# Accumulators that take turns: two column tiles of a panel, and two token halves, product by product

## What is computed

```
xn   = RMSNorm(h)
proj = xn @ w_in                 # 2048 x N_IN: three mixers (forgetting attention, gated short
                                 # convolution, gated linear attention) and three gate groups
mix  = sum_i sigmoid(g_i + b_i) * (mixer_i(proj) @ w_i_o)
h    = h + mix @ w_o
u    = causal_dwconv3(RMSNorm(h) @ w_up)          # 2048 x 11264
h    = h + (silu(u_gate) * u_up) @ w_down         # 5632 x 2048
out  = RMSNorm(h)[meta tokens dropped]
```

## Time and profile before

| | |
|---|---|
| median of the runs | 1764.99 us |
| own time of the profiled execution | 1764.8 us |
| its span | 1763.0 us |
| TensorE busy, products | 1752.1 us, 99% |
| TensorE busy, weight loads | 1694.5 us, 96% |
| VectorE, ScalarE, GpSimd busy | 64%, 43%, 9% |
| DMA, mean over the span | 180 GB/s |

### The profile page before, as it was taken

How to read it: one execution, slowest core, us unless ns; L and a number is a source line. 1 busy time by engine, 2 the same in 40 slices (tenths; PEclk the granted TensorE clock), 3 DMA queues, 4 the chain that set the end, 5 groups by cost and what they waited for, 6 DMA issues and landing times.

```text
span 1763.0 us, 34040 instructions
## 1 busy us (share of the span) xinstructions
PE 1752.1 (99%) x13509; PEld 1694.5 (96%) x13509; DVE 1125.3 (64%) x1547; ACT 763.7 (43%) x942; POOL 163.4 (9%) x318
## 2 busy tenths in 40 slices
PE   9999999999999999999999999999999999999998
PEld 8999999999999999999999999999999999888886
DVE  6757667577575554555556687777777777554454
ACT  6634444354354444444444443334444334343433
POOL 4030030300300000000000033321000000000000
PEclk9999999999999999999999999999999999999999
DMA  8656556556556556566655566666555565666564
GB/s 230 181 155 166 165 157 178 161 162 170 143 162 192 179 172 188 175 190 190 191 167 191 178 191 191 203 197 187 182 179 180 182 186 174 223 189 187 187 188 134
DMA packets 304662, 317.48 MB, mean 180 GB/s; under 512 B 13769, under 2 KB 279501, under 8 KB 304461
## 3 DMA queue, kind: packets, MB, share of 16 engines
q1 hardware_dynamic: 296861, 311.01, 58.8%
q0 software_dynamic: 7296, 4.68, 1.4%
q10 hardware_dynamic: 432, 0.79, 0.1%
HBM read 311.10 MB, written 2.11 MB: 178 GB/s over the span
## 4 chain that ended last, share of the span: by engine, by line
PE 99%; DVE 0%; DMA 0%; ACT 0%; SPq 0%; issue 0%; ACTq 0%; DVEq 0%
PE ps L1387 27%; PE ps L1389 27%; PE ps L1388 27%; PE ps L1668 5%; PE ps L1670 5%; PE ps L1669 5%; PE ps L1482 0%; DMA xb<-in_x_dram 0%; PE ps L1504 0%; PE ps L1529 0%; PE ps L1519 0%; PE ps L1520 0%; PE ps L1559 0%; PE ps L1560 0%; DVE xl L908 0%; PE ps L1547 0%
## 5 line engine op out<-in xcount | busy, mean ns | idle before, releaser
L863 DVE TENSOR_TENSOR lo<-raw,hi 128x1024 fp32r<-128x1024 f32 x584 | 711.6, 1231 | 510.2 <-ACT hi L582 507.1
L1387 PE MATMUL ps<-xh,hi 128*128 128x260 f32 (+1 forms) x3328 | 946.0, 284 | 0.2 <-DVE xl L908 0.2
L1389 PE MATMUL ps<-xh,lo 128*128 128x260 f32 (+1 forms) x3328 | 942.0, 283 | 0.0
L1388 PE MATMUL ps<-xl,hi 128*128 128x260 f32 (+1 forms) x3328 | 940.3, 283 | 0.0
L582 ACT CAST hi<-raw 128x1024 fp32r<-128x1024 f32 x584 | 604.4, 1048 | 670.5 <-PE ps L1389 539.5
L1387 PEld LDWEIGHTS ps<-xh,hi 128*128 128x128 f32 x3328 | 626.1, 188 | 1.4 <-issue 0.4
L1388 PEld LDWEIGHTS ps<-xl,hi 128*128 128x128 f32 x3328 | 626.5, 188 | 0.2
L1389 PEld LDWEIGHTS ps<-xh,lo 128*128 128x128 f32 x3328 | 625.5, 188 | 0.0
L1668 PE MATMUL ps<-hi,act_h 128*128 128x512 f32 x350 | 139.6, 399 | 0.0
L1670 PE MATMUL ps<-lo,act_h 128*128 128x512 f32 x350 | 137.9, 394 | 0.0
L1669 PE MATMUL ps<-hi,act_l 128*128 128x512 f32 x350 | 137.2, 392 | 0.0
(11 more groups left out here) (306 smaller groups left out, 1189.4 us busy)
## 6 DMA issues: line engine op xcount, KB each, us to landing
raw<-in_w_in_dram SPq DMA_DIRECT2D x224, 512.0 KB, 3.8
raw<-in_w_up_dram SPq DMA_DIRECT2D x176, 512.0 KB, 4.6
raw<-in_w_down_dram SPq DMA_DIRECT2D x88, 512.0 KB, 4.8
raw<-in_w_o_dram SPq DMA_DIRECT2D x32, 512.0 KB, 3.5
raw<-in_w_in_dram SPq DMA_DIRECT2D x32, 256.0 KB, 3.4
raw<-in_w_a_o_dram SPq DMA_DIRECT2D x16, 512.0 KB, 4.4
raw<-in_w_b_o_dram SPq DMA_DIRECT2D x16, 512.0 KB, 3.3
raw<-in_w_c_o_dram SPq DMA_DIRECT2D x16, 512.0 KB, 3.3
```

Source lines behind the costliest of these rows:

```text
L863: nc.vector.tensor_tensor(lo[:, s, :], raw[:, s, :], hi[:, s, :].bitcast(F32), ALU.subtract).then_inc(lo_ready, 1)
L1387: nc.tensor.matmul(acc, w_hi, mh, start=first and j == 0, stop=False)
L1388: nc.tensor.matmul(acc, w_hi, ml, start=False, stop=False)
L1389: ins = nc.tensor.matmul(acc, w_lo, mh, start=False, stop=last and j == KJ - 1)
```

## The change

The tiles of a column panel take turns: for each row block and each of the three products, first tile 0, then tile 1. The two first panels, which have work between their tiles, keep the old order. In the down projection the two token halves take turns in the same way, for all panels but the last four.

```diff
@@ use_panel
                 s = ph.slot(q)
-                for m in range(2):
-                    if m and between:
+                for j in () if between else range(KJ):
+                    mh, ml = moving(j)
+                    for n_, (w, mv) in enumerate(((hi, mh), (hi, ml), (lo, mh))):
+                        for m in range(2):
+                            a = 0 if m else skip
+                            ins = nc.tensor.matmul(pset(st, n)[:, m, a:], tiles(w, s, j, m), mv[:, a:], start=first and j + n_ == 0,
+                                                   stop=last and j == KJ - 1 and n_ == 2)
+                for m in range(2) if between else ():
+                    if m:
                         between()
@@ beside down_rows
+            def down_both(i, q):
+                s, st = DN.slot(q), (i * 2 + q // DQ) % 2
+                for j in range(DK):
+                    kt = (q % DQ) * DK + j
+                    w_hi, w_lo = wide(hi, s)[:, j, :], wide(lo, s)[:, j, :]
+                    for n, (act, w) in enumerate(((act_h, w_hi), (act_l, w_hi), (act_h, w_lo))):
+                        for b in range(2):
+                            ins = nc.tensor.matmul(ps[:, 2 * st + b, :], act[:, kt, b * P:(b + 1) * P], w, start=kt + n == 0,
+                                                   stop=kt == FT - 1 and n == 2)
+                return ins
@@ down_trip
-                    for b in range(2):
-                        ins = down_rows(i, q, b)
-                    ins.then_inc(panel_used, 1)
+                    down_both(i, q).then_inc(panel_used, 1)
```

## The result

The changed kernel takes 1769.57 us in the median of ten runs (1769.50 to 1771.60), the kernel before 1764.6 us in the median of ten (1764.43 to 1766.29). The ratio is 1.0029 with a 95% interval of 1.0021 to 1.0037: slower by 5.0 us. The time lies inside the predicted range of 1756 to 1774 us, but outside the 1762 to 1768 us of its likeliest case, no change.

What follows compares the result with a forecast made beforehand. The prediction took TensorE's pace of starting products to bound the kernel. Its terms added 0 to the profiled 1764.8 us; with a run median of 1764.99 it predicted 1765.0 us, range 1756 to 1774.

Steps and rivals of the forecast that it cites:

- likeliest case: Whole kernel: no change within 0.2% (3.5 us), forecast 1765.0 us, range 1762 to 1768 us, chance 0.60.
- The change of accumulator: Column panels and down projection: 11,708 more changes of accumulator, taken to cost 0, with bounds of +12 and -35 us.
- Weight loads: Column panels: the high tile is no longer loaded twice in a row; cost 0.
- Waits: Panels: waits stay at the panel's start and nobody uses the earlier finished bank, so no wait is added.
- The place and order of reads: Column panels: new neighbours among reads could move the pace up to 0.03 us per panel, -8 to +9 us; taken as 0.
- C: Column panels: slower through new neighbours among tiles, 2.89 us a panel everywhere, 1774 us; chance 0.14.
- D: Column panels: new neighbours among tiles make them faster, 2.85 us a panel, 1757 us; chance 0.13.
- A: Panels taking turns: the order removes a hand-over cost within one accumulator, 3.0 ns per product, 1730 us; chance 0.08.
- B: Panels taking turns: the whole excess over full-clock column time goes, 144 us, giving 1621 us; chance 0.02.
- E: Panels: changing banks at every product drops the clock to 1.2 GHz in stretches; 1933 us for a tenth; chance 0.01.
- F: Whole kernel: instructions could be emitted as before, so nothing changes; counted inside the no-change forecast's 0.60.
- The fixed part of 3.0 ns per product: Every product: what is left beside 0.450 ns a column; all a hand-over could give back, 35 us over all changes.

Runs made afterwards that it cites:

- e1: Kernel before with reads in the old order, but column-panel products writing to the two banks in turn: 1765.05 us, ratio 1.0001.
- e5: Kernel before with column panels' weight tiles loaded in the changed order, activations and banks as before: 1764.70 us, ratio 0.9999.
- e6: Kernel before with column panels' activations streamed in the changed order, weights and banks as before: 1769.94 us, ratio 1.0027.
- e7: Changed kernel with column tiles taking turns after three products instead of each, down projection as before: 1769.95 us, ratio 1.0030.
- e11: TensorE alone, no layer computed: blocks of 96 products in other orders of the same moving tiles; 118.4 ns a product by parts at offset 12.
- e9: TensorE alone, no layer computed: blocks of 96 products varying place, width and order; at offset 0 old order 120.1 ns a product, turns 120.4.

## Why the prediction held in its range and missed in its likeliest case

**What bounds the kernel, and how to read it.** Right: only TensorE's pace could carry the change, and it did. Durations would have misled. The mean length of a column panel's product differs by at most 1 ns between the two pages. In the down projection the first product's median length fell from 399 to 394 ns, while that stage takes 254.5 us in both kernels.

**The change of accumulator: 0 ns.** Right, and shown by e1 in both directions. The prediction's own ground was weaker than it says: it took equal lengths to bound the cost at 1 ns, but lengths moved by 5 ns without any change of pace. The steps between starts bear on it, to their rounding of 0.01 us.

**Weight loads: cost 0.** Right (e5). **Waits: none.** Right: the list of waits is the same.

**The place and order of reads: "I take 0 between them".** This is the step that failed. The term was there, with bounds of -8 and +9 us from panels of 2.85 to 2.89 us, and the sum put it at zero because nothing told its sign. It measured +5 us: gate panels went from 2.853 to 2.872 and up panels from 2.880 to 2.886, and e6 shows that the order of the moving reads does it. Nor is "what is read beside what" the point: e5 changes the neighbours among weights and activations and costs nothing. That the time lies in the range is no merit of the sum: the range had been drawn wide enough for C and D, which together had a chance of 0.27, and nothing in the argument told between them. A spread of 1% among panels with the same instructions was a signal about the pace that the sum treated as noise.

**Rival C** had the right place (column panels, the down projection untouched) and sign, and a price of twice the size, with a chance of 0.14. Half of its reason was wrong: weight tiles 512 bytes apart have no part in it (e5), and a repeated moving tile isn't the point either (e7, e11). What counts is the sequence of places from which the moving operand starts. **Rival D**, the same with the other sign, came true in one stage, the output projection, by 0.2 us. **Rivals A and B** fell with e1. **E** didn't occur: the granted clock is full in every slice. That alone wouldn't prove it, as it also reads full at the start, where the fill products of the earlier trace rows take twice as long; the unchanged pace of e1 does. That cycling through banks makes TensorE pause between groups of products, as the Trainium skill has it of a bf16 kernel (TensorE: Matmul & The Clock Gate, section "A second HAM failure mode: psum-queue depth-cycling"), no trace here shows: e1 changes banks at every product and takes the same time. **F** is out too: the products stand in the new order in the trace.

**The fixed part of 3.0 ns per product**, read off two widths, describes wide products well: by e9's block starts 320, 384 and 448 columns cost 146.7, 175.9 and 204.0 ns, where 0.450 ns a column and 3.0 give 147.0, 175.8 and 204.6. But it isn't a hand-over that another accumulator could save (e1), and for narrow products it fails. In e9, 128 and 192 columns cost (223.59 - 212.92) / 96 = 111.1 and (234.34 - 223.59) / 96 = 112.0 ns, so at the low end something other than the columns sets the pace. The Trainium skill, on the page TensorE: Matmul & The Clock Gate, section "LDWEIGHTS (loading the stationary operand)", gives P / 1.2, 106.7 ns for 128 columns, which lies 4 ns under this floor. The N / 2.4 + about 2.5 ns of the Trainium skill's same page, section "Wait — 56ns, not 53.3ns?" (110.8 for 260 columns) doesn't hold for these float32 products even with TensorE alone: 118.4 to 121.6 ns. The excess that the prediction set against that figure is real, but no accumulator can give it back.

## What to carry to other kernels

Where TensorE is the bound and its products run without a gap, compare the pace of panels that do the same work at other addresses before changing anything: a difference of 1% between them can be time to be had. Try the start column of the moving operand and the order of row blocks as free parameters, measured on TensorE alone in blocks of about a hundred products; here that foretold a full kernel to about 0.5 us, once. An order that is the best at one place can be the worse one at another, so each buffer has to be measured. Spreading this kernel's products over accumulators was neither a gain nor a loss.

## What the runs showed of the hardware that was not expected

- The start of a 260-column float32 moving tile, shifted in steps of 16 bytes over 256, changes the cost of a product between 118.4 and 121.6 ns with TensorE alone; every place at a multiple of 32 bytes from the first took 119.9 to 120.1 ns, by the distances of the block starts in e9.
- In the same way 258 columns (122.2 ns) cost more than 260 (120.0 ns) at one place, and 256 cost 118.8 ns.
- The cost depends on how often a row block is read in succession, not evenly: 118.5, 118.9, 118.9, 119.1, 119.7, 119.0 ns for 1, 2, 3, 4, 6 and 8 times at offset 12.
- The pace of an order at a place is the same to about 0.2 ns with TensorE alone and with ScalarE, VectorE and transfers at work (e9 against the kernels), and it repeats: nearly every stretch of 8 up panels of the kernel before takes 23.04 us.
